# Two transformer blocks on one core: value projections of block two as token rows at the head of each layer

## The chip, the core and the metric

The program runs on one core of a Trainium2 chip. TensorE (PE) multiplies, VectorE (DVE), ScalarE (ACT) and GpSimd (POOL) work element by element, SyncE (SP) issues the large DMAs. The metric is the device time of one launch in microseconds, the median of several runs. Lower is better.

## The reference

The input is 512 tokens of width 1024, batch 1, float32. Block one is a gated mix of sliding-window attention and a short convolution, and a gated feed-forward layer; its output passes an RMS norm. Block two has two layers, and this is where the change lies:

```python
def hybrid_layer(x, norm_gain, w_in, w_out, rel_bias, cos, sin):
    hn = rms_norm_2(x, norm_gain)
    proj = hn @ w_in                                  # 1024 -> 8 * 512
    aq, ak, av, ag, rq, rk, rv, rg = jnp.split(proj, cuts, axis=-1)
    ya = chunked_rel_attention(aq, ak, av, rel_bias)  # 8 heads of 64
    yr = chunkwise_retention(rq, rk, rv, cos, sin)    # 4 heads of 128, rotary
    y = concatenate([ya * silu(ag), yr * silu(rg)])
    return x + y @ w_out                              # 1024 -> 1024

def second_block(x, positions, norm_gain, w_in, w_out, rel_bias, final_gain):
    cos, sin = rotary_tables(positions, 128)
    for layer in range(2):
        x = hybrid_layer(x, norm_gain[layer], w_in[layer], w_out[layer], rel_bias[layer], cos, sin)
    return rms_norm_2(x, final_gain)
```

Both mixes need the values with tokens as the contracted axis: `av` times the attention weights, `rv` times the decayed scores.

## The kernel before

Everything stands transposed: a tile holds 128 features on the partitions and the 512 tokens along them. Products are made to nearly full precision from rounded parts: x is split into `x_hi` and `x_lo`, every weight tile into `w_hi` (ScalarE, line 909) and `w_lo` (VectorE, line 1277), and `products` (lines 536 to 538) makes three matmuls of 128x512 for each of the eight k tiles. A unit is one output tile of 128 features: 24 matmuls into one of four PSUM banks `main`. The units run in a fixed order: 116 for block one, then per layer of block two 32 input units (`IN2`) and 8 output units. A panel of 256 weight columns serves two units; SyncE loads it when the panel two before it has been split.

All engines walk the same list of units, each in its own written order, held together by semaphores: `unit_done` (TensorE has finished a unit), `bank_empty` (its bank has been read), `hi_ready` and `lo_ready` (weights split), `x_ready`, `y_ready` (input tiles split). The norm's factor of each token is not applied to x but to the result: TensorE sums the squares (`sum_norm`), VectorE and ScalarE take the root into `r_tok`, which holds it with tokens on the partitions, and `spread_diagonal` turns it into a row `factor`, with which VectorE multiplies every bank it reads (`apply_factor`, line 1314).

The small work of attention and retention is cut into slots. `project` runs slot 2i after half of the matmuls of unit i and slot 2i + 1 behind the unit. Slots 22 to 40 are attention (scores, turned weights, mix), slots 43 on retention (scores at line 796, mix at line 775). The order of the input units of a layer is: query 0 to 3, key 0 to 3, attention value 8 to 11, rotary query and key 12 to 19, retention value 20 to 23, gates 24 to 31. A value tile is multiplied by the factor into `v2_raw`; `turn_v` (line 594) turns it by four transposes of 128x128 into the bank `aux3`, in the middle of units 9 to 12 and 21 to 24; ScalarE copies it to `v2` or `rv` (line 1192). A rotary tile goes from VectorE to `straight`, is swapped by ScalarE, multiplied and added by GpSimd (lines 1859 and 1863), and VectorE reads the next one only when `straight` is free.

In the last stage the eight output units of layer two are made the other way round already: `row_products` (lines 865 to 867) holds 128 tokens of y still and streams 512 weight columns, four banks at a time. At the very start TensorE turns x by transposes (`turn_x`, line 657); transposes of the identity (`warm_up`, line 646) fill the time until the first data are there.

Of the kernel before, what the change touches and what calls it, by code (L numbers as in the profile page):

```python
# [25 lines left out]
F32 = mybir.dt.float32  # L26
# [27 lines left out]
IN2_PANELS = [256 * i for i in list(range(6)) + list(range(8, 14)) + [6, 7, 14, 15]]  # L54
# [66 lines left out]
def two_blocks_kernel(  # L121
# [95 lines left out]
    v2_raw = at("v2_raw", [P, 2, SEQ], F32, 16)  # L217
# [81 lines left out]
    v_turned = sem("v_turned")  # L299
    v_ready = sem("v_ready")  # L300
# [99 lines left out]

    def raw_unit(u):
        if u >= ROWS:
# [3 lines left out]
    def h_rows(half, b):  # L406
        return h[:, 4 * half:4 * half + 4, b * P:(b + 1) * P]
# [12 lines left out]
    def _(sp):  # L420
# [69 lines left out]
        for i in range(11):  # L490
# [7 lines left out]
            for j in range(2):  # L498
                dst = raw[:, n % 2, 4 * j:4 * j + 4, :].rearrange("p (k c) n -> p k (c n)", c=2)
                src = pair[j].rearrange("p k c n -> p k (c n)")  # L500
                sp.dma_start(dst, src).then_inc(raw_loaded[n % 2], 16)
        for layer in range(LAYERS):
            n0 = (IN2 + LAYER_UNITS * layer) // 2
            for i in range(16):
                projection(n0 + i, w_in_2[layer], IN2_PANELS[i])
            for i in range(4):
                if layer < LAYERS - 1:
                    projection(n0 + 16 + i, w_out_2[layer], 256 * i)
                else:
                    n = n0 + 16 + i  # L510
                    sp.wait_ge(lo_ready, 2 * n - 2)
                    for e in range(2):
                        half, pair = divmod(2 * i + e, 4)
                        sp.dma_start(raw[:, n % 2, 4 * e:4 * e + 4, :].rearrange("p (k r) c -> p k (r c)", k=2),
                                     tile_rows(w_out_2[layer], 2 * pair, 2, 512 * half, 512))\
                            .then_inc(raw_loaded[n % 2], 16)
# [12 lines left out]
    def _(pe):  # L529
# [62 lines left out]
        def turn_v(source, index, bank):  # L592
            for b in range(NB):
                done = pe.transpose(bank[:, b * P:(b + 1) * P], source[:, b * P:(b + 1) * P], ident[:])  # L594
# [45 lines left out]
        pe.wait_ge(mix_loaded, 16)  # L640
        pe.transpose(aux[3][:, 0:KT], vec_rows[0:KT, :], ident[0:KT, 0:KT]).then_inc(vec_turned, 1)
# [6 lines left out]
        warm_up(9)  # L648
# [24 lines left out]
        warm_up(9)  # L673
# [26 lines left out]
        for u in range(IN1 + FIRST_UNITS, BRANCH):  # L700
# [7 lines left out]
            if u == 8:  # L708
                pe.wait_ge(biased, 6)
                turn_v(v_raw, 0, aux[3])  # L710
# [49 lines left out]

        for layer in range(LAYERS):
# [5 lines left out]
            def ret_mix(r, layer=layer):  # L767
# [3 lines left out]
                if j == 0:  # L771
                    if n:
                        pe.wait_ge(ret_read, 4 * layer + head)
                    pe.wait_ge(v_ready, 1 + 8 * layer + 4 + head + 1)
# [1121 lines left out]
```

## Time and profile before

| | |
|---|---|
| median of 3 runs | 1255.88 us (1255.61 to 1256.25) |
| the profiled execution | 1255.21 us, span 1253.4 us |
| TensorE with a matmul | 1242.7 us (99%), 5956 matmuls |
| VectorE, ScalarE, GpSimd busy | 733.0, 530.7, 85.0 us |
| a projection matmul, 128x512 | 0.39 us |
| a weight split, ScalarE and VectorE | 1.06 and 1.24 us |
| a sum or product on GpSimd for a rotation | 1.3 us |
| retention scores times decay (VectorE), 128x512 and 128x384 | 0.69 and 0.56 us |

Matmuls overlap, so their durations add up to more than the time they take. What one is worth is the distance between two starts.

### The profile page before, as it was taken

The page shows a single profiled execution, that of the slowest core. Times are in us where ns is not written, and L with a number is a line of the kernel's source. Part 1 is how long each engine was busy: PE and PEld are TensorE (multiplying, and loading weights), DVE is VectorE, ACT ScalarE, POOL GpSimd, SP SyncE. Part 2 cuts the span into 40 slices and gives each one's busy share as a digit, 9 for nine tenths or more (in the row PEclk, how much of TensorE's full clock was granted, in tenths as well). Part 3 has the DMA queues.
Part 4 walks back from the last instruction along what each step waited for, and adds up shares of the span by engine and source line. Part 5 has one row for each costly group of instructions (what it writes and reads, how often), then busy time and mean ns, then how long its engine had stood idle before and what let it go on. Part 6 is the DMA issues. An engine that isn't in the chain of part 4 may idle for free.

```text
span 1253.4 us, 16397 instructions
## 1 busy us (share of the span) xinstructions
PE 1242.7 (99%) x5956; PEld 991.7 (79%) x5956; DVE 733.0 (58%) x1408; ACT 530.7 (42%) x878; POOL 85.0 (7%) x79
## 2 busy tenths in 40 slices
PE   8999999999999999999999999999999999999998
PEld 7888777888888888888888877777778887777776
DVE  5555774554677777776435546744654336753664
ACT  5422553444544444432324235543554235542453
POOL 3000000002000000000001001220012001220000
PEclk9999999999999999999999999999999999999999
DMA  6423222233322233323224422221124322122121
GB/s 206 121 82 101 68 68 69 100 101 101 101 87 83 98 100 100 100 101 104 83 97 135 161 69 67 68 68 49 59 95 146 114 76 68 35 68 67 68 84 67
DMA packets 102299, 114.05 MB, mean 91 GB/s; under 512 B 3801, under 2 KB 91067, under 8 KB 102107
## 3 DMA queue, kind: packets, MB, share of 16 engines
q1 hardware_dynamic: 99851, 107.68, 26.2%
q10 hardware_dynamic: 2384, 5.51, 1.2%
q8 instruction: 41, 0.67, 0.2%
q14 instruction: 23, 0.19, 0.1%
HBM read 111.04 MB, written 2.14 MB: 90 GB/s over the span
## 4 chain that ended last, share of the span: by engine, by line
PE 95%; DVE 3%; ACT 1%; issue 1%; POOL 0%; DMA 0%; DVEq 0%; ACTq 0%; POOLq 0%
PE main L536 24%; PE main L538 24%; PE main L537 24%; PE aux L626 3%; PE aux L536 3%; PE aux L538 3%; PE aux L537 3%; PE aux L605 2%; PE aux L617 2%; PE aux L796 1%; PE aux L775 1%; PE aux L566 1%; PE aux L594 1%; PE main L865 1%; PE main L867 1%
## 5 line engine op out<-in xcount | busy, mean ns | idle before, releaser
L536 PE MATMUL main<-x_hi,w_hi 128*128 128x512 f32 x1112 | 449.1, 404 | 0.5 <-DVE w_lo L1358 0.5
L538 PE MATMUL main<-x_hi,w_lo 128*128 128x512 f32 x1112 | 434.0, 390 | 0.0
L537 PE MATMUL main<-x_lo,w_hi 128*128 128x512 f32 x1112 | 433.5, 390 | 0.0
L1277 DVE TENSOR_TENSOR w_lo<-raw,w_hi 128x1024 fp32r<-128x1024 f32 x192 | 237.1, 1236 | 179.7 <-ACT w_hi L909 179.6
L909 ACT ACTIVATE w_hi<-raw 128x1024 fp32r<-128x1024 f32 x192 | 202.4, 1056 | 260.6 <-PE main L538 191.9
L536 PEld LDWEIGHTS main<-x_hi,w_hi 128*128 128x128 f32 x1112 | 209.0, 188 | 46.7 <-issue 3.6
L538 PEld LDWEIGHTS main<-x_hi,w_lo 128*128 128x128 f32 x1112 | 208.7, 188 | 45.6
L537 PEld LDWEIGHTS main<-x_lo,w_hi 128*128 128x128 f32 x1112 | 209.2, 188 | 42.7 <-issue 1.9
L1668 DVE TENSOR_TENSOR decayed<-aux,decay 128x512 f32<-128x512 f32 (+3 forms) x32 | 15.6, 489 | 65.6 <-PE aux L796 65.6
L1314 DVE TENSOR_TENSOR up_in<-main,factor 128x512 f32<-128x512 f32 x44 | 30.4, 690 | 37.9 <-PE main L538 34.9
L947 ACT ACTIVATE soft_pair<-soft_pair,neg_peak 128x256 f32<-128x256 f32 (+3 forms) x64 | 33.6, 527 | 39.8 <-DVE neg_peak L1330 39.7
L1838 POOL COPY sum_sq<-squares 128x512 f32<-128x512 f32 x4 | 2.7, 664 | 657.0 <-ACT squares L926 657.0
L1841 POOL TENSOR_TENSOR sum_sq<-sum_sq,squares 128x512 f32<-128x512 f32 x28 | 37.5, 1341 | 121.0 <-ACT squares L926 120.3
L1086 ACT ACTIVATE g_hi<-squares 128x512 f32 (+1 forms) x22 | 13.9, 632 | 65.0 <-DVE squares L1519 65.0
L1859 POOL TENSOR_TENSOR swapped<-swapped,sin_t 128x512 f32<-128x512 f32 x16 | 21.0, 1315 | 216.8 <-ACT swapped L1200 216.8
L536 PE MATMUL aux<-g_hi,w_hi 128*128 128x512 f32 x88 | 34.2, 389 | 0.0
L538 PE MATMUL main<-g_hi,w_lo 128*128 128x512 f32 x88 | 34.2, 389 | 0.0
L537 PE MATMUL aux<-g_lo,w_hi 128*128 128x512 f32 x88 | 34.2, 389 | 0.0
L538 PE MATMUL aux<-g_hi,w_lo 128*128 128x512 f32 x88 | 34.2, 389 | 0.0
L536 PE MATMUL main<-g_hi,w_hi 128*128 128x512 f32 x88 | 34.2, 389 | 0.0
L537 PE MATMUL main<-g_lo,w_hi 128*128 128x512 f32 x88 | 34.2, 389 | 0.0
L1082 ACT ACTIVATE gate_y<-gate_y 128x512 f32<-128x512 f32 x22 | 14.0, 634 | 45.5 <-DVE gate_y L1514 45.5
(248 smaller groups left out, 1738.6 us busy)
## 6 DMA issues: line engine op xcount, KB each, us to landing
raw<-in_w_in_dram SPq DMA_DIRECT2D x98, 512.0 KB, 4.4
raw<-in_w_up_dram SPq DMA_DIRECT2D x44, 512.0 KB, 3.9
raw<-in_w_out_dram SPq DMA_DIRECT2D x24, 512.0 KB, 4.0
raw<-in_w_down_dram SPq DMA_DIRECT2D x22, 512.0 KB, 4.4
rel<-band_rows ACTq DMA_DIRECT2D x2, 2048.0 KB, 9.8
x_rows<-in_x_dram SPq DMA_DIRECT2D x4, 512.0 KB, 7.4
raw<-in_w_attn_branch_dram SPq DMA_DIRECT2D x4, 512.0 KB, 3.4
raw<-in_w_conv_branch_dram SPq DMA_DIRECT2D x4, 512.0 KB, 4.3
```

What stands on the lines that cost most here:

```text
L536: pe.matmul(bank, hi, right_hi[j], start=first and j == 0, stop=False)
L537: pe.matmul(bank, hi, right_lo[j], start=False, stop=False)
L538: done = pe.matmul(bank, lo, right_hi[j], start=False, stop=last and j == len(rows) - 1)
L605: done = pe.matmul(aux[3][rows, 0:P], value(kb, half), turned[:, half, j * P:(j + 1) * P], start=j == 0, stop=j == len(blocks) - 1)
L617: done = pe.transpose(turned_block(n, half, j), soft(i, half, n * P)[:, j * P:(j + 1) * P], ident[:])
L626: pe.matmul(aux[half][:, 0:n * P], query[rows], key[rows], start=True, stop=True)\
L909: act.activation(w_hi[:, u % 4, :, :], raw_unit(u), ACT.Copy).then_inc(hi_ready, 1)
L947: act.activation(block, block, ACT.Exp, bias=negative, accum_out=total[:, i % 2, half:half + 1]).then_inc(exp_ready, 1)
L1277: dve.tensor_tensor(w_lo[:, u % 4, :, :], raw_unit(u), w_hi[:, u % 4, :, :].bitcast(F32), ALU.subtract).then_inc(lo_ready, 1)
L1314: dve.tensor_tensor(target, all_banks[main_bank(u)][:], factor[:], ALU.mult).then_inc(bank_empty, 1)
L1841: pool.tensor_tensor(sum_sq[:, 0, :], sum_sq[:, 0, :], tile, ALU.add)\
L1859: steps.then(pool.tensor_tensor(swapped[:], swapped[:], sin_t[:], ALU.mult))
```

## The change

The eight value units of a layer (attention value and retention value) come first. They are computed as token rows: 128 tokens of x are held still, 512 weight columns stream, and the results lie in the four banks `main` in the form the mixes need. A unit is two k tiles for all four token blocks; four units make one value matrix. The first and the fourth of them run block by block, the two between k tile by k tile. The norm's factor is applied while the bank is read, from `r_tok`: attention values by ScalarE, retention values by VectorE. `turn_v` is left for block one alone. The other units follow as query and key of two heads in turn, then the rotary tiles (now units 16 to 23, in the order q0 q1 k0 k1 q2 q3 k2 k3), then the gates. The norm's sum and factor keep their places or move back by one or two units, and the in-place product of `h` in layer one by four. In layer one the first two output units run with k tiles 0 to 6 each, and then both with tile 7. At the start the dummy transposes are 3, 5 and 12 in place of 9 and 9, with three of them ahead of the first wait.

```diff
-IN2_PANELS = [256 * i for i in list(range(6)) + list(range(8, 14)) + [6, 7, 14, 15]]
+VALUE_UNITS = 8
+VALUE_COLUMNS = (1024, 3072)
+IN2_PANELS = [256 * i for i in (0, 2, 1, 3, 8, 10, 9, 11, 6, 7, 14, 15)]
+
+KEY_UNITS = (10, 11, 14, 15)
+
+ROTATED_TILES = ("q0", "q1", "k0", "k1", "q2", "q3", "k2", "k3")
...
+        def rows_panel(n, w, pair, column):
+            sp.wait_ge(lo_ready, 2 * n - 2)
+            for e in range(2):
+                sp.dma_start(raw[:, n % 2, 4 * e:4 * e + 4, :].rearrange("p (k r) c -> p k (r c)", k=2),
+                             tile_rows(w, 2 * (pair + e), 2, column, 512)).then_inc(raw_loaded[n % 2], 16)
-            for i in range(16):
-                projection(n0 + i, w_in_2[layer], IN2_PANELS[i])
+            for i in range(4):
+                rows_panel(n0 + i, w_in_2[layer], 2 * (i % 2), VALUE_COLUMNS[i // 2])
+            for i in range(4, 16):
+                projection(n0 + i, w_in_2[layer], IN2_PANELS[i - 4])
...
         pe.wait_ge(ident_ready, 1)
-        pe.wait_ge(mix_loaded, 16)
-        pe.transpose(aux[3][:, 0:KT], vec_rows[0:KT, :], ident[0:KT, 0:KT]).then_inc(vec_turned, 1)
...
-        warm_up(9)
+        warm_up(3)
+        pe.wait_ge(mix_loaded, 16)
+        pe.transpose(aux[3][:, 0:KT], vec_rows[0:KT, :], ident[0:KT, 0:KT]).then_inc(vec_turned, 1)
+
+        warm_up(5)
...
         turn_x(0)
         turn_x(1)
-        warm_up(9)
+        warm_up(12)
...
-            for i in range(32):
+            def value_products(u, b, k):
+
+                bank = main[b][:]
+                hi, lo = weight_rows(u, k)
+                x, rest = [t[:, k, b * P:(b + 1) * P] for t in (x_hi, x_lo)]
+                pe.matmul(bank, x, hi, start=k == 0, stop=False)
+                pe.matmul(bank, rest, hi, start=False, stop=False)
+                return pe.matmul(bank, x, lo, start=False, stop=k == KT - 1)
+
+            for i in range(VALUE_UNITS):
+                u, pair = u0 + i, (2 * (i % 4), 2 * (i % 4) + 1)
+                pe.wait_ge(lo_ready, u + 1)
+                whole = i % 4 in (0, 3)
+                for k in pair:
+                    if i < 4:
+                        pe.wait_ge(x_ready, KT * (2 + layer) + (k + 1 if layer else 4 if k < 4 else 8))
+                    if not whole:
+                        for b in range(NB):
+                            done = value_products(u, b, k)
+                if whole:
+                    for b in range(NB):
+                        if i % 4 == 0:
+                            pe.wait_ge(bank_empty, emptied(u - 4 + b))
+                        for k in pair:
+                            done = value_products(u, b, k)
+                        if i % 4 == 3 and b < NB - 1:
+                            done.then_inc(value_rows_done, 1)
+                done.then_inc(unit_done, 1)
+                if i == 1:
+                    sum_norm((3 + layer) * KT, 2 - layer)
+                if i == 3:
+                    spread_factor(2 + 2 * layer)
+                if i == 5 and layer == 0:
+                    spread_factor(3)
+                if layer == LAYERS - 1 and i >= TURN_H:
+                    turn_h(i - TURN_H)
...
-                    if s % 2 == 0 and 9 <= s // 2 <= 12 or s % 2 == 0 and 21 <= s // 2 <= 24:
-                        t = s // 2 - 9 if s // 2 <= 12 else s // 2 - 21 + 4
-                        pe.wait_ge(bank_empty, emptied(u0 + s // 2 - 1))
-                        if t == 4:
-                            pe.wait_ge(mixed_read, 16 * (layer + 2))
-                        if t != 0:
-                            pe.wait_ge(v_ready, 1 + 8 * layer + t)
-                        turn_v(v2_raw[:, (s // 2 - 1) % 2, :], t, aux[3])
...
+                        if s < ATT2 + 16 and b == 0:
+                            pe.wait_ge(bank_empty, emptied(u0 + KEY_UNITS[t]))
...
             if layer < LAYERS - 1:
-                for i in range(8):
-                    project(u0 + 32 + i, layer, hi=y_hi, lo=y_lo, ready=y_ready, wait=i == 0,
-                            middle=spread_last if i == 0 else None)
+                for u in (u0 + 32, u0 + 33):
+                    operands_wait(u)
+                    for k in range(KT - 1):
+                        if u == u0 + 32:
+                            pe.wait_ge(y_ready, KT * layer + k + 1)
+                        products(u, main[u % 4][:], [k], [y_hi[:, k, :]], [y_lo[:, k, :]], k == 0, False)
+                        if u == u0 + 32 and k == 3:
+                            spread_last()
+                pe.wait_ge(y_ready, KT * (layer + 1))
+                for u in (u0 + 32, u0 + 33):
+                    products(u, main[u % 4][:], [KT - 1], [y_hi[:, KT - 1, :]], [y_lo[:, KT - 1, :]],
+                             False, True).then_inc(unit_done, 1)
+                for i in range(2, 8):
+                    project(u0 + 32 + i, layer, hi=y_hi, lo=y_lo)
...
+                if i == 3:
+                    act.wait_ge(root_ready, 3 + layer)
+                    for b in range(NB):
+                        if b < NB - 1:
+                            act.wait_ge(value_rows_done, 6 * layer + b + 1)
+                        else:
+                            act.wait_ge(unit_done, u + 1)
+                        act.activation(v2[:, b, :], main[b][:], ACT.Copy,
+                                       scale=r_tok[:, 1 - layer, b:b + 1]).then_inc(bank_empty, 1)
...
-                if 13 <= i < 21:
-                    rotate_straight(8 * layer + i - 13)
+                if 17 <= i < 25:
+                    rotate_straight(8 * layer + i - 17)
+                if i == 7:
+                    for b in range(NB):
+                        if b < NB - 1:
+                            dve.wait_ge(value_rows_done, 6 * layer + 3 + b + 1)
+                        else:
+                            dve.wait_ge(unit_done, u + 1)
+                        dve.tensor_scalar(rv[:, b, :], main[b][:], r_tok[:, 1 - layer, b:b + 1], None,
+                                          ALU.mult).then_inc(bank_empty, 1)
+                if i < VALUE_UNITS:
+                    pass
+                elif i < 16:
+                    t = 2 * ((i - 8) // 4) + i % 2
+                    if i % 4 < 2:
+                        apply_factor(u, q2[:, t, :], 0.125)
+                    else:
+                        apply_factor(u, k2[:, t, :])
+                elif i < 24:
+                    n = 8 * layer + i - 16
...
-                target = (rq if n % 8 < 4 else rk)[:, n % 4, :]
+                kind, head = ROTATED_TILES[n % 8]
+                target = (rq if kind == "q" else rk)[:, int(head), :]
```

TensorE, head of layer one: the last matmul of block one and the first of block two. Names are bank, operand held or streamed. Before:

```order
L537 MATMUL main3<-g_lo_104,w_hi_54 128x512
L538 MATMUL main3<-g_hi_103,w_lo_55 128x512
L536 MATMUL main0<-x_hi_57,w_hi_54 128x512
L537 MATMUL main0<-x_lo_58,w_hi_54 128x512
L538 MATMUL main0<-x_hi_57,w_lo_55 128x512
L536 MATMUL main0<-x_hi_57,w_hi_54 128x512
L537 MATMUL main0<-x_lo_58,w_hi_54 128x512
```

Now:

```order
L552 MATMUL main3<-g_lo_104,w_hi_54 128x512
L553 MATMUL main3<-g_hi_103,w_lo_55 128x512
L829 MATMUL main0<-w_hi_54,x_hi_57 128x512
L830 MATMUL main0<-w_hi_54,x_lo_58 128x512
L831 MATMUL main0<-w_lo_55,x_hi_57 128x512
L829 MATMUL main0<-w_hi_54,x_hi_57 128x512
L830 MATMUL main0<-w_hi_54,x_lo_58 128x512
L831 MATMUL main0<-w_lo_55,x_hi_57 128x512
L829 MATMUL main1<-w_hi_54,x_hi_57 128x512
L830 MATMUL main1<-w_hi_54,x_lo_58 128x512
L831 MATMUL main1<-w_lo_55,x_hi_57 128x512
```

The first unit no longer takes eight k tiles for one bank, but two k tiles for each of the four banks.

TensorE, middle of unit 22 of layer one, before, where a value tile was turned ahead of a retention mix (`rv`) and a score (`rk`):

```order
L537 MATMUL main2<-x_lo_58,w_hi_54 128x512
L538 MATMUL main2<-x_hi_57,w_lo_55 128x512
L594 MATMUL aux3<-ident_49,v2_raw_109 128x128 x4
L775 MATMUL aux2<-decayed_123,rv_113 128x512
L796 MATMUL aux1<-rq_111,rk_112 128x384
L536 MATMUL main2<-x_hi_57,w_hi_54 128x512
```

The same place now:

```order
L552 MATMUL main2<-x_lo_58,w_hi_54 128x512
L553 MATMUL main2<-x_hi_57,w_lo_55 128x512
L797 MATMUL aux2<-decayed_122,rv_112 128x512
L818 MATMUL aux1<-rq_110,rk_111 128x384
L551 MATMUL main2<-x_hi_57,w_hi_54 128x512
```

The four transposes are gone; the mix and the score stand as they did.

TensorE, end of the first output unit of layer one and beginning of the second (`main0` and `main1` are their banks), before:

```order
L538 MATMUL main0<-y_hi_124,w_lo_55 128x512
L536 MATMUL main0<-y_hi_124,w_hi_54 128x512
L537 MATMUL main0<-y_lo_125,w_hi_54 128x512
L538 MATMUL main0<-y_hi_124,w_lo_55 128x512
L536 MATMUL main1<-y_hi_124,w_hi_54 128x512
L537 MATMUL main1<-y_lo_125,w_hi_54 128x512
L538 MATMUL main1<-y_hi_124,w_lo_55 128x512
```

Now the end of tile 6 of the second unit, and tile 7 of both:

```order
L552 MATMUL main1<-y_lo_124,w_hi_54 128x512
L553 MATMUL main1<-y_hi_123,w_lo_55 128x512
L551 MATMUL main0<-y_hi_123,w_hi_54 128x512
L552 MATMUL main0<-y_lo_124,w_hi_54 128x512
L553 MATMUL main0<-y_hi_123,w_lo_55 128x512
L551 MATMUL main1<-y_hi_123,w_hi_54 128x512
L552 MATMUL main1<-y_lo_124,w_hi_54 128x512
L553 MATMUL main1<-y_hi_123,w_lo_55 128x512
```

The products of the last y tile stand 21 matmuls later than before, and those of the first unit come directly ahead of the second's.

## Rows read from the trace of the kernel before

**Rows 1.** The page: span, TensorE's busy time, its granted clock in 40 slices

```profile
span 1253.4 us, 16397 instructions
...
PE 1242.7 (99%) x5956; PEld 991.7 (79%) x5956; DVE 733.0 (58%) x1408; ACT 530.7 (42%) x878; POOL 85.0 (7%) x79
...
PEclk9999999999999999999999999999999999999999
```

**Rows 2.** TensorE's waits: line, for whom, us in total, times, longest

```profile
PE main L536 <- DVE y_lo L1713: 0.8, 1, 0.8
```

**Rows 3.** Timeline of TensorE, last stage: start us, us, instruction

```profile
1206.30 0.39 PE L865 MATMUL main<-w_hi,y_hi 128*128 128x512 f32 x1
...
1246.88 0.39 PE L867 MATMUL aux<-w_lo,y_hi 128*128 128x512 f32 x1
```

**Rows 4.** Timeline of TensorE, units 9 and 10 of layer one

```profile
729.77 0.60 PE L594 MATMUL aux<-ident,v_raw 128*128 128x128 f32 x4
730.13 0.48 PE L536 MATMUL main<-x_hi,w_hi 128*128 128x512 f32 x1
...
735.71 0.60 PE L594 MATMUL aux<-ident,v_raw 128*128 128x128 f32 x4
```

**Rows 5.** Timeline of TensorE, slots 22, 43, 44 and 45 of layer one

```profile
741.64 0.60 PE L594 MATMUL aux<-ident,v_raw 128*128 128x128 f32 x4
742.17 0.49 PE L626 MATMUL aux<-k,q 64*128 64x128 f32 x4
...
835.72 1.02 PE L796 MATMUL aux<-rq,rk 128*128 128x512 f32 x2
...
839.35 0.60 PE L594 MATMUL aux<-ident,v_raw 128*128 128x128 f32 x4
839.78 1.02 PE L775 MATMUL aux<-decayed,rv 128*128 128x512 f32 x2
...
844.03 0.81 PE L775 MATMUL aux<-decayed,rv 128*128 128x384 f32 x2
```

**Rows 6.** Timeline of TensorE and VectorE, first unit of layer one

```profile
674.66 0.39 PE L536 MATMUL main<-x_hi,w_hi 128*128 128x512 f32 x1
...
676.49 1.27 DVE L1489 TENSOR_TENSOR h<-main,h 128x512 f32<-128x512 f32 x2
...
678.52 0.39 PE L538 MATMUL main<-x_hi,w_lo 128*128 128x512 f32 x1
...
679.23 0.39 PE L537 MATMUL main<-x_lo,w_hi 128*128 128x512 f32 x1
```

**Rows 7.** Timeline of TensorE, first output unit of layer one, k tiles 5 to 7

```profile
919.28 0.40 PE L538 MATMUL main<-y_hi,w_lo 128*128 128x512 f32 x1
...
920.81 0.39 PE L537 MATMUL main<-y_lo,w_hi 128*128 128x512 f32 x1
...
921.66 0.40 PE L537 MATMUL main<-y_lo,w_hi 128*128 128x512 f32 x1
```

**Rows 8.** Timeline of TensorE, the first microseconds

```profile
2.85 2.18 PE L646 MATMUL main<-ident 128*128 128x128 f32 x9
4.83 1.91 PE L657 MATMUL aux<-ident,x_rows 128*128 128x128 f32 x8
6.54 1.29 PE L646 MATMUL main<-ident 128*128 128x128 f32 x9
8.29 0.47 PE L536 MATMUL main<-x_hi,w_hi 128*128 128x512 f32 x1 [0.47 <-DVE w_lo L1358]
```

**Rows 9.** DMA issue of the first x chunk (issued at 0.76): KB, us to landing

```profile
x_rows<-in_x_dram SPq DMA_DIRECT2D x1, 512.0 KB, 3.5
```

**Rows 10.** Timeline of VectorE and TensorE, slots 29 and 30 of layer one

```profile
776.62 0.28 DVE L1335 COPY q<-aux 128x128 f32<-128x128 f32 x1
...
777.92 0.49 PE L626 MATMUL aux<-k,q 64*128 64x128 f32 x4
```

**Rows 11.** Timeline of VectorE, a rotary tile is read behind GpSimd's sum

```profile
767.79 0.69 DVE L1314 TENSOR_TENSOR straight<-main,factor 128x512 f32<-128x512 f32 x1 [1.54 <-POOL rq L1863]
```

More of the change, by code:

```diff
@@ L509, in _ @@
                 else:
[L510 to L516, printed above, removed]
+                    rows_panel(n0 + 16 + i, w_out_2[layer], 2 * (i % 2), 512 * (i // 2))
         sp.wait_ge(rotated, 8 * LAYERS)
@@ L770, in ret_mix @@
                 pe.wait_ge(ret_decayed, n + 1)
[L771 to L774, printed above, removed]
+                if j == 0 and n:
+                    pe.wait_ge(ret_read, 4 * layer + head)
                 pe.matmul(aux[2][:, j * P:SEQ], rv[:, j, head * P:(head + 1) * P],
@@ L815, in slot @@
+            for i in range(VALUE_UNITS, 32):
+                u = u0 + i
+                def slot(s, layer=layer):
                     if ATT2 <= s < ATT2 + 19:
+                        t, b = att_step(s - ATT2)
                         if s == ATT2 and layer == LAYERS - 1:
                             pe.wait_ge(h_copied, KT)
-                        if s == ATT2 + 3:
-                            pe.wait_ge(v_ready, 1 + 8 * layer + 4)
+                        if s < ATT2 + 16 and b == 0:
+                            pe.wait_ge(bank_empty, emptied(u0 + KEY_UNITS[t]))
@@ L836, in _ @@
-                project(u, 2 + layer, order=order, wait=i == 0, middle=middle)
+                project(u, 2 + layer, middle=middle)
                 slot(2 * i + 1)
                 if layer == LAYERS - 1 and TURN_H <= i < TURN_H + KT:
-                    k = i - TURN_H
-                    if k >= 2:
-                        pe.wait_ge(h_copied, k - 1)
-                    for b in range(NB):
-                        done = pe.transpose(aux[k % 2][:, b * P:(b + 1) * P], h[:, k, b * P:(b + 1) * P],
-                                            ident[:])
-                    done.then_inc(h_turned, 1)
@@ L846, in _ @@
-                if i == 1 and layer == 0:
-                    sum_norm(3 * KT, 2)
-                if i == 2 and layer == 0:
-                    spread_factor(2)
+                    turn_h(i - TURN_H)
             def spread_last(layer=layer):
@@ L1750, in _ @@
                     apply_factor(u, gate2[:, u % 4, :])
-                if 0 < i < 31:
+                if i < 31:
                     split(u + 4)
-                if layer == 0 and 2 <= i < 10:
-                    k = i - 2
+                if i == 1:
+                    invert_norm(2 + layer, EPS2 if layer else EPS1, two=layer == 0)
+                    dve.wait_ge(root_ready, 3 + layer)
+                    make_diagonal(1 - layer)
+                if i == 4 and layer == 0:
+                    dve.wait_ge(factor_ready, 3)
+                    make_diagonal(0)
+                if i == 7 and layer:
+                    dve.wait_ge(factor_ready, 5)
+                if layer == 0 and 6 <= i < 14:
+                    k = i - 6
                     if k == 0:
```

80 lines of the change are left out of this document (28 added, 52 removed).

## The prediction, made before the changed kernel was run

> **What bounds the kernel now.** I began with the page: the span is 1253.4 us and TensorE holds a matmul in 1242.7 us of it, with its clock granted in full, at 2.4 GHz, all along [rows 1]. The list of waits says what is left: once the products have begun, the longest TensorE wait is 0.8 us for a `y_lo` tile [rows 2]. So the time is the sum of what TensorE is given, plus some stalls too short or too well hidden to be listed, which I looked for in the timeline as matmuls that start more than 0.23 us after the one before. VectorE, ScalarE and the DMA queues set the end only where they make TensorE stand still.
>
> The unit of account is the spacing of matmuls. A projection matmul lasts 0.39 us, but they overlap: in the last stage 180 of them start between 1206.30 and 1246.88, 40.58 us over 179 steps, 0.2267 us each [rows 3]. A unit of 24 is 5.44 us.
>
> **The change part by part.**
>
> *Value transposes, removed.* Each layer of block two turns eight value tiles, four transposes each: 16 groups, 64 instructions. A group is not worth its 4 x 0.27 us, since they overlap. Alone in the middle of a unit, the way from one group to the next is 735.71 - 729.77 = 5.94 us where 24 matmuls need 5.44: 0.50 us, of which only 0.36 lie in the transposes and the rest in the slower matmuls behind them [rows 4]. Six groups of the 16 stand so. Four stand ahead of attention scores, 742.17 - 741.64 = 0.53 us [rows 5]; I take 0.45 of it, an estimate, since the slow restart seen in rows 4 is paid by the scores anyway. Six stand ahead of a retention mix, 839.78 - 839.35 = 0.43 us [rows 5]. Sum: 6 x 0.50 + 4 x 0.45 + 6 x 0.43 = 7.4 us. Bounds: 64 x 0.09 (0.36 us for four, the visible part alone) = 5.8 us below, 4 x 0.53 + 12 x 0.50 = 8.1 us above.
>
> *Value products as rows, added.* Eight units per layer now hold token blocks of x still and stream the weights. The count is the same: 4 blocks x 2 k tiles x 3 = 24 matmuls of 128x512, with 24 weight loads. Their price is read from the last stage, which already multiplies this way and changes bank every three matmuls: the 0.2267 us of rows 3 are just those. Cost 0; the bound from either side is the rounding of that spacing, 384 x 0.001 = 0.4 us.
>
> *Evacuation.* Per layer VectorE loses eight factor multiplications (0.69 us each, as in [rows 11]) and gains four scaled copies; ScalarE loses eight copies and gains four. Both have idle time there, and four copies of about 0.7 us follow block by block: a block takes 6 x 0.2267 = 1.36 us, so the copies keep up, and the next unit wants the last bank only three blocks (4.1 us) after it begins. No cost; if that cover were gone, TensorE would lose at most one copy, 0.7 us, at each of four places.
>
> *Head of a layer, block by block.* Now the first unit reads all eight x tiles, and the last comes late: from 678.52 to 679.23 are 0.71 us for two steps that need 0.45, so 0.26 us are lost [rows 6]; the second layer shows the same once. After the change tiles 6 and 7 are read in the fourth unit, 16 us later. That wait goes: 0.5 us in all. What is late next is the bank of the last residual. The first unit starts at 674.66; its third block comes 12 matmuls later, 677.38. The two residual additions run 676.49 to 677.76 [rows 6], so the first of them, which frees that bank, ends at about 677.13: 0.25 us to spare, and the fourth block has 1.0. In the second layer the split and the addition together (about 3.2 us after the last unit) stand against 4.1. Cost 0, bound 0.2 per layer.
>
> *Two output units share their last y.* This is smaller than the listed wait. In unit 32 of the first layer k = 6 costs 920.81 - 919.28 = 1.53 us for two steps, 1.08 too much; k = 7 then has 921.66 - 920.81 = 0.85 for three, 0.17 too much [rows 7]. The loop still asks for y tiles 0 to 6 in unit 32 and puts off only tile 7. VectorE writes `y_lo` tile 6 behind the last head's norm and gate, in the order it had. So the 1.08 us stay and 0.17 go: 0.2 us. `unit_done` of unit 32 comes 4.8 us later, and with it the split of unit 36; that unit is needed two units (10.9 us) after the pair, and a split is 1.06 + 1.24 us. Hidden.
>
> *Dummies moved.* The first transpose waits to 2.7 us for the gain rows; nine dummies follow from 2.85, and only at 4.83 is x turned, although x, issued at 0.76, landed 3.5 us later, at 4.3 [rows 8, 9]. Nine dummies at 0.22 us stood in the way. Now three run in the wait and five behind the transpose: 2.85 + 5 x 0.22 = 3.95, so the landing decides, and the turn starts 0.5 us earlier. The first product hangs on the chain x rounding, x rest, w rest (8.29). The weight panels for units 2 and 3 come over a busy queue, so I take 0.4 us of it; bounds 0 and 0.5. Twelve dummies in place of nine end before the operands are there as long as they run at 0.11 to 0.15 us.
>
> On these dummies the page "TensorE: Matmul & The Clock Gate" of the Trainium skill (section "What's actually happening") says the default state is throttled and that activity releases it. The profile's clock row shows 1.0 from the start, but the nine dummies from 2.85 take 0.22 us each and the nine from 6.54 far less [rows 8], so the trace sides with the page against that row. By the page an earlier start of activity cannot hurt; the sum stays as it is.
>
> *Queries and keys interleaved, rotations four units later.* Same instructions. Attention slot 30 now waits in the middle of unit 15 for the key tile of unit 14, which VectorE reads behind its work for slot 29. In the old profile that work ends with the copy at 776.62 + 0.28 = 776.90; a factor read of 0.69 then ends at 777.6, and the slot starts at 777.92 [rows 10]. Margin 0.3 us: cost 0, bound 0.3 per layer.
>
> Sum: 7.4 + 0.5 + 0.2 + 0.4 = 8.5 us. The profiled execution took 1255.21 us (1.8 of it around the span); 1246.7 after. It lay 0.67 below the median of the runs, 1255.88; from there 1247.4 us.
>
> **The rivals.**
> - *Small waits eat the margins* (15 in 100). The key hand-off costs 0.3 twice, the bank at the head 0.2 twice, the start gives nothing, and the groups are worth their visible 5.8: 5.8 + 0.5 + 0.2 - 1.0 = 5.5, time 1250.4. For it: margins of 0.25 and 0.3 us. Against: VectorE and ScalarE have less to do there than before.
> - *More comes back* (8 in 100): the groups give 8.1 and the whole 1.25 of the shared y goes, because VectorE reaches the last head sooner: 8.1 + 0.5 + 1.25 + 0.5 = 10.4, time 1245.5. Against: VectorE's queue there is a serial chain that the change leaves alone.
> - *The rotations stall the retention* (2 in 100, the other side). Units 20 to 23 now wait for GpSimd's sum inside VectorE's queue (1.54 us idle before a read [rows 11]), and behind it stand `w_lo` and the `decayed` product for which the mix waits. From slot 43 (835.72) VectorE has 0.4 + 0.69 + 0.69 + 1.3 + 0.69 + 1.23 + 0.56, 5.6 us, until the next `decayed`, and the mix of slot 45 asks 8.3 us after slot 43 [rows 5], 7.9 without the transposes: 2.3 us of room. It decides from there: with the chain at 10 us each of eight places would lose 2.1, 16.8 in all, and the time would be 1264.
> - *The clock falls where banks change* (1 in 100). At 1.2 GHz in place of 2.4 the 384 value matmuls would take twice their 0.2267 us: +87 us, 1334. Against: the last stage changes banks and keeps 0.2267. The same page, "A second HAM failure mode: psum-queue depth-cycling", reports a kernel whose cycling through banks made the clock swing. Rows 3 do not show it here.
> - *No gain* (4 in 100): a queue that I did not see takes the freed time back, such as the raw panels, now in 2 KB pieces and another order.
>
> **How the numbers follow.** Forecast 70 in 100: 1247.4, its own range 1246 to 1249. With the two nearest rivals 1245.5 to 1250.5. Less than about 0.2% (2.5 us) could not be told from no change. Faster by more than that: the forecast and the first two rivals, 0.93; the same 0.04; slower 0.03.
>
> **What would show it.** Right: no transposes between units 9 and 24 of either layer; from the first value matmul to unit 32 each layer some 3.9 us shorter; value matmuls at 0.227 us; no step over 0.3 us in the first unit of a layer; the first product near 7.9 us; before `y_lo` tile 6 still a wait of about 1 us. Wrong: a wait for a `v` or `rv` copy, a key tile or `decayed`, or value matmuls wider than 0.23 us.

## The result, and the profile after

The changed kernel takes 1247.02 us (median of 4 runs, 1246.86 to 1247.19), the kernel before took 1255.75 us beside it (4 runs, 1255.61 to 1256.25). The ratio is 0.993, with a 95% interval of 0.9913 to 0.9947. The forecast was 1247.4. The profiled execution took 1247.10 us in place of 1255.21, 8.1 less, and the span is 1245.3 in place of 1253.4.

The page of the profile, in the parts shown in [rows 1], then one of its groups (busy us and mean ns behind the bar):

```profile
span 1245.3 us, 16231 instructions
...
PE 1235.4 (99%) x5894; PEld 986.2 (79%) x5894; DVE 725.6 (58%) x1400; ACT 525.7 (42%) x870; POOL 85.3 (7%) x79
...
PEclk9999999999999999999999999999999999999999
...
L829 PE MATMUL main<-w_hi,x_hi 128*128 128x512 f32 x128 | 50.5, 394 | 0.0
```

TensorE is still the bound. It has 62 matmul records fewer (64 transposes went and two dummies came) and 7.3 us less busy time, and a matmul of the value rows (lines 829 to 831) lasts 0.39 us like every other projection matmul. The waits of TensorE after the change, to be read beside [rows 2]:

```profile
PE main L659 <- POOL ident L1874: 2.1, 1, 2.1
PE main L551 <- DVE y_lo L1760: 0.8, 1, 0.8
PE aux L581 <- DVE rq L1704: 0.4, 2, 0.2
...
```

The two rows left out are 0.2 us each, for the first DMA and for a norm's sum. No wait for a copy of `v` or `rv`, for a key tile or for `decayed` is among them, and the 0.8 for `y_lo` is still there. The 2.1 us for `ident` stand where the kernel before waited 2.7 us for the gain rows, ahead of all products. So none of the freed time was handed to a new wait of any size. To see where the 8.1 us came from, the span is cut at points that both kernels have. Before, at the norm's sums in block one (33.38) and in layer one (685.84), at the first product of y in each layer, and at the last matmul in [rows 3]:

```profile
33.38 0.94 PE L566 MATMUL aux<-mean,sum_sq 128*128 128x1 f32 x8
...
685.84 1.39 PE L566 MATMUL aux<-mean,sum_sq 128*128 128x1 f32 x12
...
914.92 0.39 PE L536 MATMUL main<-y_hi,w_hi 128*128 128x512 f32 x1
...
1202.80 0.39 PE L865 MATMUL main<-w_hi,y_hi 128*128 128x512 f32 x1
```

The same points after:

```profile
33.67 0.95 PE L581 MATMUL aux<-mean,sum_sq 128*128 128x1 f32 x8
...
685.86 1.39 PE L581 MATMUL aux<-mean,sum_sq 128*128 128x1 f32 x12
...
911.05 0.39 PE L551 MATMUL main<-y_hi,w_hi 128*128 128x512 f32 x1
...
1194.68 0.39 PE L908 MATMUL main<-w_hi,y_hi 128*128 128x512 f32 x1
...
1238.77 0.39 PE L910 MATMUL aux<-w_lo,y_hi 128*128 128x512 f32 x1
```

| stretch | before | after | difference |
|---|---|---|---|
| start to the sum in block one | 33.38 | 33.67 | +0.29 |
| to the sum in layer one (holds the head of layer one) | 652.46 | 652.19 | -0.27 |
| to the first y product of layer one | 229.08 | 225.19 | -3.89 |
| to the first y product of layer two | 287.88 | 283.63 | -4.25 |
| to the last matmul | 44.08 | 44.09 | +0.01 |

Both layers give about the same, the head of layer one gives the 0.26 of [rows 6], the last stage gives nothing, and the start took 0.29 us more where 0.4 less was forecast. The last four stretches add up to 1213.50 us before and 1205.10 after, 8.4 less. They repeat closely: in the seven profiles of the changed kernel and of its variants that differ only in the start, their sum lies between 1205.07 and 1205.14.

### The profile page after: what moved, and what is told of

It is laid out like the page before. It is cut to its first block, busy times and chain, and to the rows that moved or that the text cites. A ratio compares the mean times of both kernels' runs of the same rounds, so it can differ in the third digit from the quotient of the medians.

```text
span 1245.3 us, 16231 instructions
## 1 busy us (share of the span) xinstructions
PE 1235.4 (99%) x5894; PEld 986.2 (79%) x5894; DVE 725.6 (58%) x1400; ACT 525.7 (42%) x870; POOL 85.3 (7%) x79
## 4 chain that ended last, share of the span: by engine, by line
PE 96%; DVE 2%; issue 1%; ACT 0%; POOL 0%; DMA 0%; DVEq 0%; ACTq 0%; POOLq 0%
PE main L551 22%; PE main L553 22%; PE main L552 22%; PE aux L641 3%; PE aux L551 3%; PE aux L552 3%; PE aux L553 3%; PE aux L620 2%; PE main L829 2%; PE main L831 2%; PE main L830 2%; PE aux L632 2%; PE aux L818 1%; PE aux L797 1%; PE aux L581 1%; PE main L908 1%
## 5 line engine op out<-in xcount | busy, mean ns | idle before, releaser
L551 PE MATMUL main<-x_hi,w_hi 128*128 128x512 f32 x984 | 397.7, 404 | 0.0
L553 PE MATMUL main<-x_hi,w_lo 128*128 128x512 f32 x984 | 384.0, 390 | 0.0
L552 PE MATMUL main<-x_lo,w_hi 128*128 128x512 f32 x984 | 383.5, 390 | 0.0
L551 PEld LDWEIGHTS main<-x_hi,w_hi 128*128 128x128 f32 x984 | 184.9, 188 | 40.5 <-issue 3.4
L553 PEld LDWEIGHTS main<-x_hi,w_lo 128*128 128x128 f32 x984 | 184.7, 188 | 40.2
L552 PEld LDWEIGHTS main<-x_lo,w_hi 128*128 128x128 f32 x984 | 185.1, 188 | 38.0 <-issue 1.9
L829 PE MATMUL main<-w_hi,x_hi 128*128 128x512 f32 x128 | 50.5, 394 | 0.0
L831 PE MATMUL main<-w_lo,x_hi 128*128 128x512 f32 x128 | 49.9, 390 | 0.0
L830 PE MATMUL main<-w_hi,x_lo 128*128 128x512 f32 x128 | 49.9, 390 | 0.0
```

The lines of the kernel that those rows point to most:

```text
L551: pe.matmul(bank, hi, right_hi[j], start=first and j == 0, stop=False)
L552: pe.matmul(bank, hi, right_lo[j], start=False, stop=False)
L553: done = pe.matmul(bank, lo, right_hi[j], start=False, stop=last and j == len(rows) - 1)
L829: pe.matmul(bank, x, hi, start=k == 0, stop=False)
L830: pe.matmul(bank, rest, hi, start=False, stop=False)
L831: return pe.matmul(bank, x, lo, start=False, stop=k == KT - 1)
```

## The experiments

Each experiment is the changed kernel with one edit, the last with two. Two of the runs are the changed kernel itself: `again`, 1247.14 us (1246.77 to 1247.74), on one chip with `k_by_k`, `y_undone` and `tail_blocks`, and `again_2`, 1247.09 us (1246.77 to 1247.95), on one chip with `old_start_2` and `no_dummies`. The other four (`turns_back`, `old_start`, `six_dummies`, `two_y_late`) ran on a third chip, where only the kernel before stood beside them; it took 1256.07 us there and 1256.00 beside `again`, so the distance to `again` holds to about 0.1 us and the scatter of the medians.

**The transposes back, with nothing to carry.** Four transposes of the identity into the bank `aux3` stand again at each of the 16 places in the middle of the units.

```diff
+                    if s in (18, 20, 22, 24, 42, 44, 46, 48):
+                        if s == 18:
+                            pe.wait_ge(factor_ready, 4 + layer)
+                        if s == 42:
+                            pe.wait_ge(mixed_read, 16 * (layer + 2))
+                        for b in range(NB):
+                            pe.transpose(aux[3][:, b * P:(b + 1) * P], ident[:], ident[:])
```

> The changed kernel with four transposes of the identity put back at each of the sixteen old places (middle of units 9 to 12 and 21 to 24 of both layers); their result is read by nobody. Theory A (the time is the sum of what TensorE is given): 6 x 0.50 + 4 x 0.45 + 6 x 0.43 = 7.4 us longer than the changed kernel's 1247.0, so 1254.4. Rival B (the gain came from the VectorE and ScalarE work that left, or from waits on them): these stay away, so 1247 to 1249.

Measured: 1254.05 us (1253.69 to 1255.1), 6.9 above `again`; against the kernel before 0.9984 (0.9975 to 0.9993). Its first y products stand at these times:

```profile
915.43 0.39 PE L551 MATMUL main<-y_hi,w_hi 128*128 128x512 f32 x1
...
1202.68 0.39 PE L915 MATMUL main<-w_hi,y_hi 128*128 128x512 f32 x1
```

Its norm sum of layer one is at 686.65, so layer one has 228.78 us (3.59 more than after), and from there to layer two are 287.25 (3.62 more): 7.2 us for 16 groups, 0.45 each. Two groups of `turns_back` in a row:

```profile
730.37 0.60 PE L872 MATMUL aux<-ident 128*128 128x128 f32 x4
...
736.30 0.60 PE L872 MATMUL aux<-ident 128*128 128x128 f32 x4
```

From group to group 5.93 us for 24 matmuls that need 5.44: 0.49, the 0.50 of [rows 4]. The transposes alone carry seven eighths of the 8.1 us that the trace shows. The rival, that the gain came from the work of VectorE and ScalarE, is out: that work stayed away here and the time came back.

**The first value unit k tile by k tile.** It takes all four banks for k tile 0 and then all four for k tile 1.

```diff
-                whole = i % 4 in (0, 3)
+                whole = i % 4 == 3
...
                     if not whole:
                         for b in range(NB):
+                            if i % 4 == 0 and k == 0:
+                                pe.wait_ge(bank_empty, emptied(u - 4 + b))
                             done = value_products(u, b, k)
```

> The changed kernel with the first value unit of each layer made k tile by k tile, so that all four banks are wanted within 2.0 us instead of 4.1. Theory A (the bank of the last residual is late next): bank four is free at 677.8 and is wanted at 677.0 in layer one, and in layer two at 3.2 against 2.0 us; with the restart 0.9 and 1.3 us of waits, 2.2 us slower than the changed kernel. Rival B (the order within the unit is worth nothing, the gain at the head is from the x tiles alone): the same time.

Measured: 1249.75 us (1249.56 to 1250.32), 2.6 above `again`. The stall stands where the third bank is wanted, six matmuls into the layer. TensorE there, in `k_by_k`:

```profile
675.67 0.39 PE L831 MATMUL main<-w_lo,x_hi 128*128 128x512 f32 x1
...
677.11 0.50 PE L829 MATMUL main<-w_hi,x_hi 128*128 128x512 f32 x1 [1.05 <-DVE h L1538]
```

TensorE and VectorE at the same place after the change:

```profile
676.78 1.27 DVE L1536 TENSOR_TENSOR h<-main,h 128x512 f32<-128x512 f32 x2
...
677.67 0.40 PE L829 MATMUL main<-w_hi,x_hi 128*128 128x512 f32 x1
```

The first of the two residual additions ends at about 676.78 + 0.64 = 677.42, and block by block the third bank is wanted at 677.67. The margin is 0.25 us, as forecast. K tile by k tile it is wanted 1.36 us earlier, and the stall, with the slower step behind it, costs about as much in each layer: 1.41 us in the stretch with the head of layer one, 1.46 in that of layer two, 2.9 together. The expectation had 0.9 and 1.3; the place was right, the price too low. So the order inside this one unit is worth 2.6 us by the medians and 2.9 in the trace: it is a condition of the change, not a term of its gain, since the kernel before had no such wait to remove.

**The shared y undone.** Unit 32 takes all eight tiles of y, then unit 33.

```diff
-                for u in (u0 + 32, u0 + 33):
-                    operands_wait(u)
-                    for k in range(KT - 1):
...
-                for i in range(2, 8):
-                    project(u0 + 32 + i, layer, hi=y_hi, lo=y_lo)
+                for i in range(8):
+                    project(u0 + 32 + i, layer, hi=y_hi, lo=y_lo, ready=y_ready, wait=i == 0,
+                            middle=spread_last if i == 0 else None)
```

> The changed kernel with the first two output units of layer one as before: each with all eight y tiles. Theory A (only the 0.17 us for tile 7 went): 0.2 us slower than the changed kernel, below what can be told, and in the trace tile 6 costs 1.07 us too much and tile 7 about 0.17. Rival B (the shared y is worth the whole listed wait): 1.0 us slower or more.

Measured: 1247.30 us (1246.97 to 1247.84), 0.16 above `again`; by the medians alone that is inside the scatter. In the trace the way from the first y product of layer one to that of layer two is 283.78 us in place of 283.63, and the rows have the place. TensorE in `y_undone`, the last matmul of k tile 6 and the first two of k tile 7:

```profile
917.17 0.40 PE L553 MATMUL main<-y_hi,w_lo 128*128 128x512 f32 x1
917.44 0.50 PE L551 MATMUL main<-y_hi,w_hi 128*128 128x512 f32 x1
917.78 0.39 PE L552 MATMUL main<-y_lo,w_hi 128*128 128x512 f32 x1
```

From 917.17 to 917.78 are 0.61 us for two steps that need 0.45: 0.16 lost at tile 7. TensorE and VectorE there after the change, to be read beside [rows 7]:

```profile
915.42 0.40 PE L553 MATMUL main<-y_hi,w_lo 128*128 128x512 f32 x1
915.87 0.68 DVE L1760 TENSOR_TENSOR y_lo<-gate,y_hi 128x512 fp32r<-128x512 f32 x1
916.60 0.50 PE L551 MATMUL main<-y_hi,w_hi 128*128 128x512 f32 x1 [0.79 <-DVE y_lo L1760]
...
916.94 0.39 PE L552 MATMUL main<-y_lo,w_hi 128*128 128x512 f32 x1
```

916.94 - 915.42 = 1.52 us for two steps: the 1.08 too much at tile 6 has stayed to within a hundredth, and only tile 7 was put off.

**Tiles 6 and 7 put off, not tile 7 alone.**

```diff
-                    for k in range(KT - 1):
+                    for k in range(KT - 2):
...
-                    products(u, main[u % 4][:], [KT - 1], [y_hi[:, KT - 1, :]], [y_lo[:, KT - 1, :]],
-                             False, True).then_inc(unit_done, 1)
+                    products(u, main[u % 4][:], [KT - 2, KT - 1], [y_hi[:, k, :] for k in (KT - 2, KT - 1)],
+                             [y_lo[:, k, :] for k in (KT - 2, KT - 1)], False, True).then_inc(unit_done, 1)
```

> The changed kernel with y tiles 6 and 7, not 7 alone, put off to behind the first six tiles of the first two output units of layer one. Theory A (the wait of 1.07 us is for tile 6, which VectorE writes behind the last head's norm): that wait goes, 1.0 us shorter, 1246.0. Rival B (the wait only moves, to the split weights or the bank of a later unit): no difference, 1247.0.

Measured: 1246.26 us (1246.07 to 1247.14), ratio to the kernel before 0.9925 (0.9911 to 0.9938). The wait for `y_lo` is gone from TensorE's list of waits, and the way from the first y product of layer one to that of layer two is 282.52 us (911.25 to 1193.77) in place of 283.63: 1.1 less, the whole stall.

**The start.** The old order of dummies and the wait for the gain rows, in two separate sets of runs:

```diff
-        warm_up(3)
         pe.wait_ge(mix_loaded, 16)
         pe.transpose(aux[3][:, 0:KT], vec_rows[0:KT, :], ident[0:KT, 0:KT]).then_inc(vec_turned, 1)

-        warm_up(5)
+        warm_up(9)
...
-        warm_up(12)
+        warm_up(9)
```

> The changed kernel with the start of the kernel before (9 and 9 dummies, none ahead of the first wait). Theory A (in the profile of the changed kernel the twelve dummies after x ran slowly and held the first product to 8.60 us, against 8.29 before; when the clock rises differs from run to run): within 0.4 us of the changed kernel on either side, and in its profile the first product near 8.3. Rival B (moved dummies bring the 0.4 us of the prediction in most runs): 0.4 us slower than the changed kernel, 1247.4.

Measured: 1247.62 us (1247.08 to 1247.9). In the same set stood the change with six dummies in place of the twelve (`warm_up(6)`):

> The changed kernel with six dummies in place of twelve after the turn of x. Theory A (dummies at the slow rate hold the first product back): first product at about 7.95 us, 0.65 earlier than in the changed kernel's profile, and the time 0.3 to 0.7 us shorter, 1246.3 to 1246.7. Rival B (fewer dummies leave TensorE idle and it reaches its full rate later, so that the first products take 0.45 in place of 0.23 us each): the first products slower, and the time the same or up to 2 us longer.

Measured: 1247.43 us (1247.06 to 1248.02). The first product came earlier than in the changed kernel's profile, and no gain can be seen. TensorE in `six_dummies`:

```profile
7.78 0.47 PE L551 MATMUL main<-x_hi,w_hi 128*128 128x512 f32 x1 [0.28 <-DVE w_lo L1405]
...
10.84 0.47 PE L551 MATMUL main<-x_hi,w_hi 128*128 128x512 f32 x1 [1.43 <-DVE w_lo L1405]
```

Six matmuls later it stood for 1.43 us, since ScalarE waited for a weight panel. ScalarE there:

```profile
9.34 1.15 ACT L1016 ACTIVATE w_hi<-raw 128x512 fp32r<-128x512 f32 x2 [1.56 <-DMA raw<-in_w_in_dram]
```

The half panel issued at 1.80 us landed 7.5 us after its issue here. The same transfer took 6.1 in the profiles of before and after, and 5.6 to 7.4 in the others. Over the eleven profiles of the changed kernel and its variants that have dummies, the norm sum of block one goes with that landing: with 5.6 to 6.3 us it starts between 33.20 and 33.67, with 6.8 at 33.84 (`two_y_late`), with 7.0 at 33.99 (`old_start_2`), with 7.4 at 34.42 and 34.41 (`old_start` and `turns_back`, whose dummies differ), with 7.5 at 34.57 (`six_dummies`). No run changed the landing by itself, but the late starts go with it and not with the dummies. Which theory is right can't be read from one such start, so the old order was run again on the same chip as the changed kernel, with a kernel without any dummies (the three `warm_up` calls taken out):

The run `again` had been expected to put the first product anywhere from 7.9 to 8.9 us, against the rival that 8.6 belongs to the program. It came at 8.21.

> The changed kernel as partner of the two starts of this call. Theory A: ratio 0.993 to the kernel before; the first products hang on the landing of the weight half for units 2 and 3 and on when the dummies become fast, so that the norm sum (the first matmul with sum_sq) begins anywhere between 33.2 and 34.6 us.

> The changed kernel with the old start, once more, beside the changed kernel. Theory A (the landing of the weights bounds the start in most runs, so that earlier dummies give back little): 0 to 0.4 us slower than the changed kernel, spreads overlapping. Rival B (the moved dummies bring nothing or cost, as the profile of the changed kernel alone would say): equal or up to 0.3 us faster.

> The changed kernel with no dummy transposes at all: TensorE waits for the gain rows, then for x, then for the first operands. Theory A (the dummies let TensorE reach its fast rate before the products): x is turned at 4.3 us as before, the first product at about 7.8 us, but products take 0.43 us from start to start for some microseconds, and the time is 0.5 to 3 us longer than the changed kernel's. Rival B (the landing of the weights hides that): the same time within 0.3 us.

Measured: `again_2` 1247.09 us, `old_start_2` 1247.03 us (1246.8 to 1247.51), `no_dummies` 1248.37 us (1247.98 to 1248.7). In this pair moving the dummies is worth nothing; with the first set, where the old order was 0.48 above the changed kernel of another set, it lies between -0.1 and +0.5. All runs together point to the upper half of that. The time of a launch less the four stretches behind the norm sum of block one is the start, with 6.5 us behind the last matmul and 1.8 around the span, which are the same in both: 1256.03 - 1213.50 = 42.5 us for the kernel before (median of 37 runs), 1247.47 - 1205.1 = 42.4 for the two runs of the old order (10 executions), 1247.09 - 1205.1 = 42.0 for the changed kernel (14 executions). Single executions of one kernel lie up to 1.5 us apart (1255.12 to 1256.63), so this is an estimate of 0.4 us for the moved dummies, and no proof. Having dummies at all is worth 1.3 us. TensorE in `no_dummies`:

```profile
8.21 0.77 PE L551 MATMUL main<-x_hi,w_hi 128*128 128x512 f32 x1 [1.55 <-DVE w_lo L1402]
8.78 0.63 PE L552 MATMUL main<-x_lo,w_hi 128*128 128x512 f32 x1
9.20 0.63 PE L553 MATMUL main<-x_hi,w_lo 128*128 128x512 f32 x1
...
11.76 0.41 PE L553 MATMUL main<-x_hi,w_lo 128*128 128x512 f32 x1
12.01 0.40 PE L551 MATMUL main<-x_hi,w_hi 128*128 128x512 f32 x1
```

Its first product is as early as in `again` (8.21), but its products start 0.43 us apart from the second on until 11.76, and 0.23 apart from then on. The nine steps from 8.21 to 12.01 take 3.80 us against 2.04, 1.76 lost, a part of which the other kernels lose to operands that are late.

**Both heads improved.** `two_y_late`, and in the last stage the first row unit block by block as well (line 918 on):

```diff
                 for b in range(NB):
-                    if k == 0 and v == 0:
-                        pe.wait_ge(bank_empty, emptied(ROWS - NB + b))
-                    done = row_products(v, b, k)
-                if v == 0 and k == 0:
-                    spread_last()
+                    if v:
+                        done = row_products(v, b, k)
+            if v == 0:
+                for b in range(NB):
+                    pe.wait_ge(bank_empty, emptied(ROWS - NB + b))
+                    for k in (0, 1):
+                        done = row_products(v, b, k)
+                    if b == 1:
+                        spread_last()
```

> The kernel two_y_late with the first row unit of the last stage made block by block as well. Theory A (there the last gate's bank holds up the fourth block by 0.3 us): 0.3 us less than two_y_late, so 1.3 us less than the changed kernel of this call, 1245.7. Rival B (the norm spread of the last head then comes too late for tile 7 and a wait takes its place): the same as two_y_late or up to 0.5 us slower.

Measured: 1245.52 us (1245.43 to 1246.29), ratio to the kernel before 0.9919 (0.9906 to 0.9933): the best of all, 1.6 below `again`. The last stage takes 43.83 us (1193.27 to 1237.10) in place of 44.09. After the change TensorE still had this step at the fourth bank of that stage:

```profile
1196.49 0.39 PE L910 MATMUL main<-w_lo,y_hi 128*128 128x512 f32 x1
1196.91 0.50 PE L908 MATMUL main<-w_hi,y_hi 128*128 128x512 f32 x1
1197.25 0.40 PE L909 MATMUL main<-w_hi,y_lo 128*128 128x512 f32 x1
```

0.76 us for two steps that need 0.45; block by block it is gone. The 1.1 us of the y tiles and the 0.26 of the last stage make 1.4; the remaining 0.3 of the 1.6 is within what two kernels' medians scatter.

## Why the prediction was right, point by point

**The transposes, 7.4 us.** Right, 0.2 to 0.5 too high. Put back they cost 7.2 us in the trace and 6.9 in the medians. That rules out the visible part alone (5.8) and the upper bound (8.1). The restart behind a group is a real part of its price.

**The value products, 0.** Right. The rows run at the 0.2267 us of [rows 3]. TensorE at the end of the sixth unit of layer one and in the seventh and eighth:

```profile
709.77 0.40 PE L831 MATMUL main<-w_lo,x_hi 128*128 128x512 f32 x1
...
710.48 0.40 PE L829 MATMUL main<-w_hi,x_hi 128*128 128x512 f32 x1
...
714.38 0.39 PE L831 MATMUL main<-w_lo,x_hi 128*128 128x512 f32 x1
...
719.82 0.39 PE L831 MATMUL main<-w_lo,x_hi 128*128 128x512 f32 x1
```

From 714.38 to 719.82 are 24 steps and 5.44 us. The rival of a clock that falls where banks change is out: the steps would be twice as wide, and the clock row shows full speed, 2.4 GHz, all along. What the Trainium skill reports of a clock that swings when a kernel cycles through banks ("TensorE: Matmul & The Clock Gate", section "A second HAM failure mode: psum-queue depth-cycling") did not happen here, at 0.227 us a matmul.

**The evacuation, 0.** Right: no wait of TensorE for a bank or a copy.

**The heads, 0.5.** Right: -0.27 in layer one for the 0.26 of [rows 6]. In layer two the kernel before took 0.72 us for the two steps from 964.77, and after the change its first value unit has no step over 0.3 us. The bank margin of 0.25 us was read rightly too, and `k_by_k` shows what stood behind it.

**The shared y, 0.2.** Right: 0.16, and the larger wait stayed because the loop still asks for tile 6.

**The key tile of unit 14.** Right, with 0.1 us more room than thought. VectorE and TensorE, slots 29 and 30, to be read beside [rows 10]:

```profile
774.51 0.28 DVE L1382 COPY q<-aux 128x128 f32<-128x128 f32 x1
774.71 0.68 DVE L1361 TENSOR_TENSOR k<-main,factor 128x512 f32<-128x512 f32 x1
...
775.81 0.49 PE L641 MATMUL aux<-k,q 64*128 64x128 f32 x4
```

The tile is done at 775.39 and is wanted at 775.81. The retention did not stall either, so the rival on the other side is out as well.

**The dummies, 0.4.** The size is open, the way to it was wrong. The prediction put the first product near 7.9 and said that twelve dummies end in time "as long as they run at 0.11 to 0.15 us". In the profiled run they did not. TensorE after the change, to be read beside [rows 8]:

```profile
4.53 1.97 PE L674 MATMUL aux<-ident,x_rows 128*128 128x128 f32 x8
6.29 2.56 PE L659 MATMUL main<-ident 128*128 128x128 f32 x12
8.60 0.48 PE L551 MATMUL main<-x_hi,w_hi 128*128 128x512 f32 x1
```

x was turned 0.3 us earlier than before, but the twelve dummies took 2.56 us, 0.21 each for most of them, and held the first product to 8.60 without any wait for an operand. In `again_2` the same twelve took 1.47 us and the first product came at 7.83, after a wait of 0.39 for `w_lo`:

```profile
5.96 1.47 PE L659 MATMUL main<-ident 128*128 128x128 f32 x12
7.83 0.47 PE L551 MATMUL main<-x_hi,w_hi 128*128 128x512 f32 x1 [0.39 <-DVE w_lo L1405]
```

And an early first product is not what counts: in `six_dummies` it came at 7.78 and the norm sum of block one at 34.57, after the change at 8.60 and 33.67. The step that failed is that a time saved ahead of the first product was taken as a time saved. In the traces the end of this stage goes with how late the weight half panel issued at 1.80 us lands. Even so the 0.4 may be about right: the pair of profiles lost 0.3 us at the start, but the profiled execution before, 1255.21, was one of the fastest of its kernel (the lowest of 37 is 1255.12), and by the medians of all runs the start takes 42.5 us before and 42.0 after. If so, the number came out without the reason given for it.

**What the sum missed.** Layer one gave 3.89 us, the transposes alone 3.59. The other 0.3 us is for the most part a stall at a factor spread. TensorE in layer one before:

```profile
696.15 0.39 PE L538 MATMUL main<-x_hi,w_lo 128*128 128x512 f32 x1
696.55 0.50 PE L580 MATMUL aux<-diag_hi,ones 128*128 128x512 f32 x1
...
697.11 0.39 PE L536 MATMUL main<-x_hi,w_hi 128*128 128x512 f32 x1
```

That is 0.96 us from 696.15 to 697.11, and after the change 0.71 (709.77 to 710.48, in the rows above): 0.25 less. The trace has the cause: before, the weight load for this spread stood for 0.43 us until VectorE's `diag_lo` (line 1307, 695.35 to 696.49) was done. The spread stands behind the sixth unit now instead of in the middle of the fourth, and `diag_lo` ends at 709.17, ahead of the 710.00 at which it is wanted. With the transposes back (`turns_back`) the way is 0.71 as well, so this gain doesn't hang on them. The stretch to the first y product of layer two gave 4.25 us; less 3.62 for the transposes, 0.26 for its head and 0.15 for the shared y, 0.2 remain, for which no single row was found.

**The sum.** In the trace the terms are 7.2 (transposes), 0.5 (heads), 0.2 (shared y), -0.3 (start) and 0.5 (the 0.3 and 0.2 that were not foreseen), together 8.1; since the last term is what the others leave, the sum can't help closing. The forecast had 8.5, and the medians, 1255.75 and 1247.02, differ by 8.7. Of the 0.6 us between trace and medians 0.5 come from the profiled execution before, which lay that far below the median beside it. So the total is in part luck: transposes 0.2 too high, 0.5 us not foreseen, and a start that lost 0.3 us in the profiled pair and gained about 0.4 by the medians of all runs.

## What to carry to other kernels

Small TensorE work in the middle of a stream of matmuls costs its visible time and a restart: the distance between two such places, less the matmuls between them, is its price, and it forecast a gain of 7 us to within 0.5. When a layout change removes such work, the order inside the first unit decides whether the banks are free; ask of each reordering which bank is wanted how many matmuls earlier. When a stall is to be hidden by putting a tile off, look which tile the stall stands at: here the one before it had the 1.1 us.

## What the runs showed of the hardware that was not expected

- The first microseconds differ from run to run of one kernel. The same twelve dummies took 2.56 us once and 1.47 once, and the same weight transfer landed 5.6 to 7.5 us after its issue. In the twelve profiles of the changed kernel and its variants the norm sum of block one starts between 33.20 and 34.91 us (before: 33.38); the latest is the kernel without dummies, of the rest the late ones go with a late landing of that transfer and not with the order of the dummies. So one pair of profiles can't tell what a change of the start is worth: a transfer that lands 1.4 us later (6.1 and 7.5) moves the stage by more than the change under test.
- In `no_dummies` TensorE's first products run at half their later rate, and the granted clock does not tell it. For the products of `no_dummies` 0.43 us apart, at 8.30 to 11.70 us, the row of the stretch has 1.00, full speed, in its third column from the end (TensorE's busy time and matmuls stand second):

```profile
8.30:11.70 3.40, 3.40 (x8) 2.70 (x9) 2.98 (x6) 1.15 (x2) 0.00 (x0) 1.00 1.08 382
```

The same holds for the dummies of the changed kernel, 0.21 us apart at first and 0.11 later. The rule of the Trainium skill that the default state is throttled and that activity releases it ("TensorE: Matmul & The Clock Gate", section "What's actually happening") agrees with these distances, and not with the 1.00 of the clock column; that the clock is the cause is inferred from the factor of two (0.43 to 0.23), no run here shows it directly.
